# The last projection block of a hybrid decoder layer split by token groups, with its own PSUM banks for the first output tile

## The reference

```python
proj = x @ w_in + b_in                                # 1024 -> 2*384 + 256 + 3*384
a_val, a_gate, u_b, c_bg, c_cg, c_h = split(proj)
a  = silu(layer_norm(causal_dwconv([st_a, a_val * sigmoid(a_gate)], 31 taps) + bias))
bo = multiscale_pool([st_b, u_b]) @ w_pool * pool_scale     # windows 2, 4, 8, 16, minus the token
co = c_bg * causal_dwconv([st_c, c_cg * c_h], 3 taps)       # short gated conv
m  = concat(a, bo, co) @ w_out + b_out
x1 = layer_norm(ALPHA * x + m)                        # LN1
y  = sum over the 2 chosen of 16 experts: gate * ((silu(x1 @ w_gate) * (x1 @ w_up)) @ w_down)
out = layer_norm(ALPHA * x1 + y)                      # LN2
```

## Time and profile before

| what | value |
|---|---|
| runs | 917.54, 916.64, 916.65 us |
| median | 916.65 us |
| profiled execution | 917.25 us, span 915.6 us |
| PE busy | 825.1 us, 90% |
| DVE busy | 587.5 us, 64% |
| ACT busy | 441.9 us, 48% |
| POOL busy | 266.2 us, 29% |
| last projection block, until | 240.7 us |
| first output tile starts | 251.7 us |

### The profile page before, as it was taken

How to read it: one execution, slowest core, us unless ns; L and a number is a source line. 1 busy time by engine, 2 the same in 40 slices (tenths; PEclk the granted TensorE clock), 3 DMA queues, 4 the chain that set the end, 5 groups by cost and what they waited for, 6 DMA issues and landing times.

```text
span 915.6 us, 12783 instructions
## 1 busy us (share of the span) xinstructions
PE 825.1 (90%) x4275; PEld 718.1 (78%) x4276; DVE 587.5 (64%) x732; ACT 441.9 (48%) x494; POOL 266.2 (29%) x259
## 2 busy tenths in 40 slices
PE   5999999999599999459999999999999999999900
PEld 5999999998488887338888888888888888888800
DVE  4069999966276555697998894139821523937138
ACT  5122232435723312518889885248922734846233
POOL 3333465472000000023434343123412322333225
PEclk9999999999899999659999999999999999999955
DMA  8211111103608432549999999329972572983164
GB/s 284 52 42 40 41 42 46 45 24 112 236 33 312 161 115 98 138 134 311 377 394 391 371 396 359 51 63 357 394 234 62 163 216 59 360 279 87 32 227 175
DMA packets 59407, 167.34 MB, mean 183 GB/s; under 512 B 6757, under 2 KB 25190, under 8 KB 55286
## 3 DMA queue, kind: packets, MB, share of 16 engines
q1 hardware_dynamic: 51318, 144.57, 42.4%
q0 software_dynamic: 8064, 22.45, 11.5%
HBM read 144.79 MB, written 28.24 MB: 189 GB/s over the span
## 4 chain that ended last, share of the span: by engine, by line
PE 64%; DVE 6%; DMA 2%; ACT 1%; issue 1%; POOL 0%; POOLq 0%; ACTq 0%; DVEq 0%
PE PS L1505 31%; PE PS L1521 16%; PE PS L1435 11%; PE PS L1282 5%; DVE C L1062 1%; PE PS L1411 1%; DVE RAW L1259 1%; DMA sum_rows<-F,MIX 1%; DMA F<-x_rows,MIX 0%; DMA RAW<-sum_rows 0%; DVE RAW L1183 0%; DVE RAW L1276 0%; ACT MIX L860 0%; DVE BIG L381 0%; DVE C L1064 0%
## 5 line engine op out<-in xcount | busy, mean ns | idle before, releaser
L1505 PE MATMUL PS<-BIG,TH 128*128 128x512 f32 x1248 | 295.7, 393 | 1.5 <-DVE TH L1218 1.5
L1505 PEld LDWEIGHTS PS<-BIG,TH 128*128 128x128 f32 x1248 | 233.5, 189 | 49.3 <-issue 1.9
L1303 PE MATMUL PS<-BIG,WD 128*128 128x352 f32 x1224 | 205.2, 328 | 3.1 <-DVE BIG L997 3.1
L1303 PEld LDWEIGHTS PS<-BIG,WD 128*128 128x128 f32 x1224 | 200.7, 190 | 4.8 <-DVE BIG L997 3.2
L322 DVE TENSOR_TENSOR BIG<-RAW,BIG 128x2048 fp32r<-128x2048 f32 x64 | 145.1, 2288 | 24.3 <-ACT BIG L894 24.3
L1521 PE MATMUL PS<-WD,TH 128*128 128x512 f32 x624 | 156.2, 399 | 0.0
L1521 PEld LDWEIGHTS PS<-WD,TH 128*128 128x128 f32 x624 | 113.5, 189 | 22.3
L894 ACT ACTIVATE BIG<-RAW 128x2048 fp32r<-128x2048 f32 x64 | 119.0, 1908 | 15.4 <-PE PS L1435 7.9
L292 DVE SCALAR_TENSOR_TENSOR PS<-RAW,C,PS 128x512 f32<-128x512 f32 x174 | 115.3, 745 | 0.0
L1435 PE MATMUL PS<-BIG,WD 128*128 128x512 f32 (+1 forms) x432 | 102.0, 396 | 11.0 <-DVE BIG L381 11.0
L1435 PEld LDWEIGHTS PS<-BIG,WD 128*128 128x128 f32 (+1 forms) x432 | 78.1, 182 | 31.9 <-issue 11.2
(11 more groups left out here) (198 smaller groups left out, 742.1 us busy)
## 6 DMA issues: line engine op xcount, KB each, us to landing
RAW<-in_w_gate SPq DMA_DIRECT2D x64, 512.0 KB, 7.3
RAW<-in_w_up SPq DMA_DIRECT2D x64, 512.0 KB, 8.7
MIX<-in_w_down SPq DMA_DIRECT2D x32, 1024.0 KB, 9.9
F<-in_w_in SPq DMA_DIRECT2D x17, 512.0 KB, 4.1
F<-in_x_prompt SPq DMA_DIRECT2D x10, 512.0 KB, 4.9
x_rows<-F SPq DMA_DIRECT2D x9, 512.0 KB, 2.7
sum_rows<-F SPq DMA_DIRECT2D x9, 512.0 KB, 3.6
RAW<-in_w_out SPq DMA_DIRECT2D x4, 1024.0 KB, 6.1
```

The lines of the kernel that those rows point to most:

```text
L1303: mm = pe.matmul(bank(3 * q + g, GRP), win[:, q, ws, c, :], xT[:, xs_, c, g * GRP:(g + 1) * GRP], start=(c == 0 and ws + xs_ == 0), stop=( ...
L1505: mm = pe.matmul(bank(h), xe[:, xs_, c, :], w, start=(c == 0 and xs_ + ws == 0), stop=(c == KD - 1 and xs_ == 1))
```

## The change

It has these parts.
- The last block (`project_last`) does token group 0 first, 24 matmuls over all eight chunks, signals `first_group`, does the pool products p00 and p10, and then goes through the chunks again for groups 1 and 2. The jobs b01, b2, and the other pool products stand between those chunks. The list `jobs` has p00 and p10 ahead of b01 and b2.
- `short_mul` can be done for some groups alone: of the last block, group 0 waits for `first_group` only; groups 1 and 2 come after the first two w_out units on VectorE.
- ScalarE's order after `deviation(2)`: swish 0 and 1, pool copies 0, mix copy 0, state rows b, swish 2, pool copies 1 and 2, w_out units 0 and 1, mix copy 1, w_out units 2 and 3.
- Output tile 0 (and every even tile) uses the banks 3 and 7, odd tiles 0 and 1. Tile 0 waits for all pool copies and the short products of the block before last, tile 1 for those of the last.
- The staging rows `out_b`, `out_ap`, `out_c` move from RAW into F2 (the former gate buffer and the one behind it). ScalarE waits for `short_conv` (POOL's last use of it) ahead of the copy a3.
- SP loads the w_out units 2 and 3 after the b2 transpose, ahead of the b stores; the wait for the stores now stands ahead of the LN1 rows.

The diff, cut:

```diff
-        out_b = RAW[:, OFF_B:OFF_B + 3 * WB].rearrange("p (s n) -> p s n", s=3)
-        out_ap, out_c = (RAW[:, OFF_B + 3 * WB + 272 + i * WA:OFF_B + 3 * WB + 272 + (i + 1) * WA] for i in range(2))
+        out_b = F2[:, 0:3 * WB].rearrange("p (s n) -> p s n", s=3)
+        out_ap, out_c = (F2[:, TOK + i * WA:TOK + (i + 1) * WA] for i in range(2))
...
-                   ("b01", "state_out_bc", 4), ("b2", "state_out_bc", 5)]
-                + [(f"p{c}{g}", "pool_out", CB * g + c + 1) for g in range(3) for c in range(CB)])
+                   ("p00", "pool_out", 1), ("p10", "pool_out", 2), ("b01", "state_out_bc", 4), ("b2", "state_out_bc", 5)]
+                + [(f"p{c}{g}", "pool_out", CB * g + c + 1) for g in range(1, 3) for c in range(CB)])
...
+        def out_bank(i, h):
+            return ((3, 7), (0, 1))[i % 2][h]
...
@@ sync @@
+            misc_ready(sp, "b2")
+            load_wo(2)
+            sp.wait_ge(S("tap_products"), CC)
+            load_wo(3)
             sp.wait_ge(S("state_out_bc"), 5)
             for b in range(DECB):
                 ...
             sp.dma_start(nb_p[0, 0], out_b[0:HB, 2, :]).then_inc(S("state_stored_bc"), 16)
-            sp.wait_ge(S("tap_products"), CC)
-            sp.wait_ge(S("state_stored_bc"), 16 * (2 * DECB + 3))
-            load_wo(2)
-            load_wo(3)
             sp.wait_ge(S("win_lo"), NCH)
             sp.wait_ge(S("state_stored_a"), 16 * DECB)
+            sp.wait_ge(S("state_stored_bc"), 16 * (2 * DECB + 3))
...
@@ scalar @@
             state_a(2)
+            act.wait_ge(S("short_conv"), 2 * CC)
             state_a(3)
...
             deviation(2)
-            state_b()
-            for g in range(3):
-                pool_outs(g)
...
             swish(0)
+            swish(1)
+            pool_outs(0)
+            mix_hi(0)
+            state_b()
+            swish(2)
+            pool_outs(1)
+            pool_outs(2)
             wo_hi(0)
-            swish(1)
             wo_hi(1)
-            swish(2)
-            mix_hi(0)
+            mix_hi(1)
             wo_hi(2)
             wo_hi(3)
-            mix_hi(1)
...
@@ vector @@
-            short_mul(2)
+            short_mul(2, (0,))

             mix_lo(dve, 0)
-            for u in range(4):
-                wo_lo(dve, u)
+            wo_lo(dve, 0)
+            wo_lo(dve, 1)
+            short_mul(2, (1, 2))
             mix_lo(dve, 1)
+            wo_lo(dve, 2)
+            wo_lo(dve, 3)
...
@@ tensor @@
+            def project_last():
+
+                pe.wait_ge(S("win_lo"), NCH)
+                between = {1: (state("b01", CB, lambda c: sequences(bS, c, 0, nb0),
+                                     lambda c: sequences(bS, c, nb0, DECB - nb0)),),
+                           2: (state("b2", CB, lambda c: bP[:, c, SEQ:]),),
+                           3: (pool_linear(0, 1), pool_linear(1, 1)), 4: (pool_linear(0, 2), pool_linear(1, 2))}
+                for groups in ((0,), (1, 2)):
+                    for c in range(KD):
+                        if groups[0]:
+                            for small in between.get(c, ()):
+                                small()
+                        for ws, xs_ in ((0, 0), (0, 1), (1, 0)):
+                            for g in groups:
+                                mm = pe.matmul(bank(g, GRP), win[:, 0, ws, c, :], xT[:, xs_, c, g * GRP:(g + 1) * GRP],
+                                               start=(c == 0 and ws + xs_ == 0), stop=(c == KD - 1 and ws == 1))
+                        if groups[0] and c in (1, 3, 5):
+                            mm.then_inc(S("xT_used"), 1)
+                    if not groups[0]:
+                        mm.then_inc(S("first_group"), 1)
+                        pool_linear(0, 0)()
+                        pool_linear(1, 0)()
+                mm.then_inc(S("multiplied"), 1)
...
             for i in range(NT):
                 M = rows_of(i)
                 pe.wait_ge(S("mix_lo"), i + 1)
+                if i == 0:
+                    pe.wait_ge(S("pool_out"), 3 * CB)
+                    pe.wait_ge(S("short_done"), 3 * (CC - 1))
+                if i == 1:
+                    pe.wait_ge(S("short_done"), 3 * CC)
```

More of the change, by code:

```diff
@@ L1035, in norm_a, with short_mul @@
                     dve.tensor_tensor(m, m, stdev[g], ALU.mult).then_inc(S("ln_a_norm"), 1)
-            def short_mul(c):
-                dve.wait_ge(S("multiplied"), N_BG + c + 1)
+            def short_mul(c, groups=range(3)):
                 dve.wait_ge(S("short_conv"), 2 * (c + 1))
-                for g in range(3):
+                for g in groups:
+                    if c == CC - 1 and g == 0:
+                        dve.wait_ge(S("first_group"), 1)
+                    else:
+                        dve.wait_ge(S("multiplied"), N_BG + c + 1)
                     m = mix[:, 5 + c, g * GRP:(g + 1) * GRP]
@@ L1087, in _ @@
                 for h in range(2):
-                    dve.tensor_tensor(r[:, h * 512:(h + 1) * 512], bank(2 * (i % 2) + h, rows=M),
+                    dve.tensor_tensor(r[:, h * 512:(h + 1) * 512], bank(out_bank(i, h), rows=M),
                                       r[:, h * 512:(h + 1) * 512], ALU.add).then_inc(S("out_taken"), 1)
@@ L1396, in _ @@
             pe.wait_ge(S("short_done"), 3)
[L1397 to L1401, removed]
+            def project_last():
[10 more added lines that the diff above has]
+                        for ws, xs_ in ((0, 0), (0, 1), (1, 0)):
+                            for g in groups:
+                                mm = pe.matmul(bank(g, GRP), win[:, 0, ws, c, :], xT[:, xs_, c, g * GRP:(g + 1) * GRP],
[7 more added lines that the diff above has]
+                mm.then_inc(S("multiplied"), 1)
+            project_last()
             def route(i):
@@ L1434, in _ @@
                         for h in range(2):
-                            mm = pe.matmul(bank(2 * (i % 2) + h, rows=M), mhl[:, i % 2, ms, c, 0:M],
+                            mm = pe.matmul(bank(out_bank(i, h), rows=M), mhl[:, i % 2, ms, c, 0:M],
                                            wo[:, ws, c, h * 512:(h + 1) * 512],
```

## The result

The changed kernel takes 905.96 us (median of 4 runs, 904.88 to 906.62) against 916.64 for the kernel before (4 runs), a gain of 10.7 us in the medians where 10.6 was forecast. The ratio worked out for these runs is 0.9875, with a 95% interval of 0.9859 to 0.9892, which is 11.5 us (9.9 to 12.9); it is not the quotient of the two medians (0.9883), which lies in the interval. The profiled execution took 906.62, span 904.8, against 917.25 and 915.6.

What follows compares the result with a forecast made beforehand. TensorE was taken as the bound, its expert stream only to begin earlier. Tile 0 taken at 254.05 instead of 264.62 gains 10.6: 917.25 - 10.6 = 906.65, less 0.6 for the median, 906.1; range 904.9 to 909.0.

Steps and rivals of the forecast that it cites:

- The bound and the place: TensorE bounds; the full expert stream can only begin earlier, time can be won before output tile 0.
- the hole: TensorE's 10.95 us without work between last projection block and output tile 0, forecast to shrink to under 1.
- ScalarE's and VectorE's steps: Summed job times from the last block to tile 0: start 241.5, taken by VectorE 254.05 against 264.62.
- The second stop: TensorE's wait inside tile 0 before w_out unit 2, forecast at about 1.1 us.
- the drain: About 1.38 us beside ScalarE's 1.28 table load before the early swishes; with it, a gain of 10.0.
- a sign of being wrong: VectorE waiting for x rows at line 1096, pool copies 2 ending after 237.3, or a longer routing stretch.
- The split block: Rival: three successive matmuls into one bank in group 0 don't overlap, 0.156 more each; 913.6, chance 0.04.
- my 0.175: Forecast us per matmul in the last projection block; group 0's 24 take 4.2.
- The stores and the x rows: SP's store wait ends 240.5, x block near 247.5; rival of late rows: 914.5, or 918.5 if slower, chance 0.06.
- The clock: At tile 0, staying at full through the short stops; about 1.5 us of the 10.6 gain.
- the rival of the falling clock: The clock falls all the same at tile 0's short stops, price 1.5 us; time 907.6, chance 0.09.
- The swing from small idles: Skill's claim that frequent small idles between matmul groups swing the clock to half; it would make the 0.09 clock rival likely.

Runs made afterwards that it cites:

- the second profile: The changed kernel measured again, unchanged, on the same chip as the follow-up runs: 907.23 us, ratio 0.9881 to the kernel before.
- the better order: Changed kernel with w_out unit 0 ahead of ScalarE's pool copies 2, and VectorE's w_out parts ahead of short products 1, 2 and mix part 1: 903.36 us.
- the filled hole: Kernel before with 47 small filler matmuls of constants into an unused bank before output tile 0: 914.93 us, ratio 0.9972.
- 40 fillers: Kernel before with 40 small filler matmuls of constants into an unused bank before output tile 0: 916.04 us, ratio 0.9981.
- the clock brought up before: The w_out-unit-0-first order on the changed kernel, plus 16 filler matmuls between the routing table's sum and the gate products: 902.08 us, ratio 0.9828.

## Why the prediction was right

*The bound and the place.* Right: everything behind tile 0 moved as a block, the hole was ScalarE's order, and both the order undone (917.2, no gain) and the order alone (4.5 us) say so. It was the order and the split together: without the split about 5 us are missing.

*ScalarE's and VectorE's steps.* Taken from the block's start (the forecast's 224.6, which the trace has at 224.75), the forecast and what came: first mix copy begins 6.2, came 6.1; last pool copies end 12.6, came 12.6; w_out unit 0 starts tile 0 at 16.9, came 16.9; tile 0 taken 29.4, came 29.2. The second stop was 0.73 instead of 1.1. The table load of 1.28 us had swish 0.02 behind it; the drain that the Trainium skill states (ScalarE: Activation LUTs, What ACT_TABLE_LOAD costs) does not show here either. The gain in this stretch is 10.7, forecast 10.6. The stretch from the first taking to the first expert product, which I had called a sign of being wrong if it grew, was 0.3 us longer in this pair and 0.1 in the second profile.

*The split block.* The rival fell: 24 matmuls three in a row into one bank took 3.84 us to the next start, 0.160 each, slightly less than my 0.175.

*The stores and the x rows.* This step was mis-sized, with no effect on the time. I had the stores done 15.9 us after the block's start and the first x block there after 22.9; SP's wait ended after 17.5 (4.3 us of it behind the w_out loads) and the block came after 26.1. VectorE did wait, 0.63 us, where I had named that as a sign of being wrong; 1.8 us were left before the tile's result, so it cost nothing. In the better order this slack is used up.

*The clock.* The gain from it was put about right (1.5; the filled hole gave 1.7 in its trace), but not for the right reason. I took from the earlier trace rows that over 3 us without work leave the clock at full. That was one stop: in the run without the split it fell about 2.3 us after TensorE's last matmul, and with 40 fillers at the end of a stop of 2.03. The two stops of 1.01 and 0.73 kept it, in both profiles of the changed kernel, and so did the one of 1.88. So the rival of the falling clock was nearer than I had it, and its price was too low as well. Two tiles at full clock take 22.0 us, not the 2 x 11.15 of my sum, in which the end of a tile's last matmul is counted beside the start of the next. The kernel before lost 1.7 against this, being at half for 3.6 us behind the tile's start (up to 255.3 us); with the order alone it was 2.7 for 5.6 us, with the old banks 2.8 for 5.9. The swing from small idles, which the Trainium skill describes (TensorE: Matmul & The Clock Gate, A second HAM failure mode: psum-queue depth-cycling), did not occur at these stops: the granted clock was 1.00 throughout.

*The medians.* The forecast 906.05 and the median 905.96 agree better than the method deserves: the changed kernel measured again gave 907.23, and the start of the program, the first expert tile and the wait near 530 us each vary by 1.5 us or more from one execution to the next.

## What to carry to other kernels

When an engine waits for a chain that crosses two others, look first at the order in which the feeding engine does its jobs: work for later consumers (here swish for tokens of later tiles, ahead of the weights for the first) is the cheapest thing to move. Own buffers and finer pieces bring nothing until that is done, and then, here, they brought as much again and more, since each removes the wait that comes next. A hole in TensorE's work can cost more than its length: behind each of the stops of 2.0 to 11.5 us at this place the next two tiles took 1.5 to 2.8 us longer at half clock, behind those of 1.0 us and less nothing.

## What the runs showed of the hardware that was not expected

- How far into a stop the granted clock fell differed from profile to profile: about 2.3 us in the run without the split (0.63 on average from 243 to 244, last matmul ended at 241.03), while the kernel before was still at full after 3.3. Behind 9.1 us of small fillers it fell at the end of a stop of 2.03. A stop of 1.88, and stops of 1.01 and 0.73 a few microseconds apart, left it alone.
- What it costs goes by how long the clock stays at half behind the start of the work, not by the length of the stop: 1.7 us for a stop of 10.95, 2.8 for one of 4.31.
- The same code reached the last block at 222.6 to 224.75 us. The late starts are those with the longer stretch at half clock in the first 27 us.
- The same 42 matmuls at the start of the expert stage took 11.15 to 12.71 us in twelve profiles of kernels that differ in nothing near them, and 9.84 with the clock brought up before. Two executions of one kernel gave 12.71 and 11.31. A stop of 1.6 to 2.6 us in the expert stream, at 528 to 540 us, stood in three of thirteen profiles, whatever the kernel.
- The nine stores of 15 KB issued behind 2 MB of loads held their issuer 4.3 us after the last of them, 2.0 us longer than the loads needed to land (7.3 us after issue at the latest, at 238.6; the DMA share from 238 to 240 was 0.08). With nothing ahead, before the change and in the run with the old loads, they took 1.1. What holds them beyond the loads stays open.
